# Draining the compressed heads between three projection jobs, letting the first group of heads run on into the second, and dealing the second gate's sums 2, 3, 3, 3, 3, 2

## The chip, the core and the metric

The kernel runs on one core of one Trainium2 chip. The metric is device time in microseconds. Three runs of the kernel before gave 1657.56 us (median), 1658.36 us and 1652.24 us. What a measurement of this kernel can tell from no change is about 0.5%, some 8 us.

## The reference, cut to what matters

One step of a transformer trunk over 128 context tokens and 256 latent tokens (three tiles of 128 rows), width 2048:

```
sh1, sc1, g1, sh2, sc2, g2 = split(silu(cond) @ w_mod + b_mod, 6)        # per condition
z   = modulate(rms_norm(x, g_attn), sh1, sc1) @ w_in                     # one wide projection
A:  6 heads, softmax over all latent keys and the context keys
B:  6 heads, softmax over a band of latent keys, the context keys and a sink
C:  4 heads over a low-rank compressed key/value ("compressed heads")
x   = x + g1 * (concat(o_a, o_b, o_c) @ w_o)
x   = x + g2 * moe(modulate(rms_norm(x, g_ffn), sh2, sc2))               # 32 experts, top 2
```

The six parts of the modulation each take a 2048 x 2048 slice of `w_mod` (16 MB in float32). The change concerns when the attention of C, A and B is drained, and when the slices for the gate g1 (G1), the scale sc2 (SC2) and the gate g2 (G2) are worked off.

## The kernel before, in words

The order of the work is written out by the function `plan()`, which returns one list of steps. Every engine then walks that same list and does its own part of each step; semaphores tie the engines together. An engine never takes a later step before an earlier one, so the place of a step in the list is its place in the queue of each engine.

The kinds of step that matter here:

- `proj`: a projection job, one column chunk of `w_in` for one tile of 128 tokens. TensorE (PE) does 16 matmuls in the program, shown as 32 by the profile (L1263). ScalarE (ACT) squares and copies the result out of the bank and raises `z_ready`; GpSimd (POOL) forms the factor of the norm (L2546, L2498) and raises `rstd_ready`.
- `norm`: VectorE (DVE) scales the job's columns by norm and gain (L2167) and, for latent tiles, rotates them (L1962 to L1967), then raises `norm_ready`.
- `turn`, `cache`: PE transposes the job's result, or the cached keys, into one of two transpose banks (L1304, L1310), and ACT copies them out and raises `tp_read`.
- `qk`: scores of one head and tile (L1323 and L1325 for C, L1329 for A and B); DVE takes the maximum (L2222), ACT the exponential (L1753). `nz`: DVE normalises the probabilities (L2236, L2237). `pt`: PE transposes them into a transpose bank (L1337), ACT copies them out (L1763, L1768).
- `pv`: PE multiplies by the values (L1354). For a compressed head the result goes into the last quarter of the very transpose bank that the same head's `pt` used, and DVE copies it out from there (L2244) and raises `o_ready`. For A and B three heads share one `pv` and a bank of their own (L2246).
- `mod`: PE adds one of the 16 slices of G1 or SC2 (L1121), 1 MB of weights each. After the 16th DVE adds the bias row (L2151), and the first slice of the next part waits for that. `sum`: DVE adds a slice of sh2 itself (L2132). `g2`: DVE adds a slice of G2 itself (L2108).
- `lead`: a quarter of the first tile of the output projection, dealt between the last attention steps. `out`: one tile and column block of the output projection (L1239).

The two transpose banks are used in turn. The function `tp_bank` lets PE into a bank when ACT has read what was there two uses ago; and where that was the `pt` of a compressed head, also when DVE has copied that head's output:

```python
                if n - 2 in output_in:
                    pe.wait_ge(o_ready, pv_units.index(output_in[n - 2]) + 1)
```

Inside `plan()`, `advance(u)` moves the attention pipeline by one: `qk` of a new unit u, then a waiting `pv`, `nz` and `pt` of older ones; `advance()` without a unit drains it by one. `attend(...)` calls it for a list of heads and tiles, with `mod` steps dealt in by `before`, `before_pt`, `before_pv` and `drain`. `mods(n)` takes the next n slices from `later`, a list of 16 of G1 and 16 of SC2.

Weights come by one DMA queue on SyncE, 1 MB units into a ring of 12 slots, in the order in which `plan()` lists them; a unit is requested when the unit 12 places before it has been used. After the attention come the output projection, the router, and the experts in pairs; the loop over pairs (L1533, L1564) fills the time from about 748 us to the end.

Of the kernel before, what the change touches and what calls it, by code (L numbers as in the profile page):

```python
# [26 lines left out]
TILES = 3  # L27
T = TILES * P
KD = D // P
HD = 128  # L30
HEADS_A, HEADS_B, HEADS_C = 6, 6, 4
SHARE = 3
# [83 lines left out]
LATER_GROUPS = (G1, SC2)  # L116
SUMMED = {"aq0": (0, 1, 1), "aq1": (1, 1, 1), "bq0": (1, 1, 1), "akv": (2, 2, 2), "bq1": (1, 1, 0)}
FOLD_LOW = 12
G2_STEPS = (3, 3, 2, 3, 2, 3)
SCALED_AT = {6: (0, 1, 2), 7: (3, 4, 5), 8: (6, 7, 8), 9: (9,), 10: (10,), 11: (11,)}  # L120
FOLD_AT = 6

# [70 lines left out]
def plan():  # L193
# [18 lines left out]
    def mod(g, k):  # L212
        if g == "lead":
            if k == 0:
                units.extend([("out", 0, i) for i in range(4)])
            steps.append((g, k))
            return
        units.append(("mod", g, k))
        if (g, k) == (G1, FOLD_LOW):
            steps.append(("fold", 1))  # L220
        steps.append(("mod", g, k))
# [8 lines left out]
    later = [(g, k) for g in LATER_GROUPS for k in range(KD)]  # L230
    pending = []
    summed = [0]

    def job(kind, what, norm=True):
        jobs.append(what)
        if what == ("akv", 0):
            steps.append(("fold", 0))
        steps.append((kind, len(jobs) - 1))
        for _ in range(SUMMED[what[0]][what[1]] if what[0] in SUMMED else 0):
            units.append(("mod", SH2, summed[0]))  # L240
            steps.append(("sum", summed[0]))
            summed[0] += 1
        if norm:
            steps.append(("norm", len(jobs) - 1))
        if len(pending) == 2:
            steps.append(("turn", pending.pop(0)))
        pending.append(len(jobs) - 1)
# [4 lines left out]
    scored, unnormalised, turned_p = [], [], []  # L252

    def advance(u=None, fill=0, before_pv=0):

        if u is not None:
            steps.append(("qk", u))
            scored.append(u)
        if turned_p:
            mods(before_pv)  # L260
            steps.append(("pv", turned_p.pop()))
        if unnormalised:
            steps.append(("nz", unnormalised.pop()))
        if u is not None:
            unnormalised.append(u)
        if scored and (u is None or len(scored) > 2):
            if unnormalised == [scored[0]]:
                steps.append(("nz", unnormalised.pop()))
            mods(fill)
            done = scored.pop(0)  # L270
            steps.append(("pt", done))
            if atts[done][0] == "C" or atts[done][1] % SHARE == SHARE - 1:
                turned_p.append(done)

    def attend(group, heads, tiles=range(TILES), fill=(), flush=False, drain=(), before=(), before_pt=(), before_pv=()):

        fill = list(fill)
        each = [(h, t) for h in heads for t in tiles] if group == "C" else [(h, t) for t in tiles for h in heads]
        drain = list(drain)
        for n, (h, t) in enumerate(each):  # L280
            if fill:
                mod(*fill.pop(0))
            mods(before[n] if n < len(before) else 0)
            atts.append((group, h, t))
            advance(len(atts) - 1, before_pt[n] if n < len(before_pt) else 0, before_pv[n] if n < len(before_pv) else 0)
        while flush and (scored or turned_p):
            mods(drain.pop(0) if drain else 0)
            advance()

    def mods(n):  # L290
        for g, k in later[:n]:
            mod(g, k)
        del later[:n]
# [3 lines left out]
    def chunk_units(name):  # L297
        units.extend(units_of(name))
# [16 lines left out]
    for name, _, _ in CHUNKS:  # L315
        if name in EARLY + ("cq1", "aq0"):
            continue
        chunk_units(name)
        for t in range(TILES):
            attends = name in ("aq1", "bq1", "bkv") or (name, t) == ("bq0", 0)  # L320
            job("proj", (name, t), norm=not attends)
            n = len(jobs) - 1
            if name == "akv" and t == 0:
                steps.append(("cache", "a"))
            if name == "aq1":
                attend("C", [t])
            if (name, t) == ("bq0", 0):
                attend("C", [TILES], flush=True, drain=(1, 1, 1))
            if name == "bq1":
                if t == 0:  # L330
                    steps.append(("turn", pending.pop(0)))
                    attend("A", range(SHARE), [t], before=(1, 0, 1))
                else:
                    attend("A", range(SHARE), [t], before_pt=(0, 1), before_pv=(0, 0, 1))
            if name == "bkv":
                attend("A", range(SHARE, HEADS_A), [t], before_pt=(0, 1), before_pv=(0, 0, 1))
            if attends:
                steps.append(("norm", n))
    for n in (1, 1, 0):
        mods(n)  # L340
        advance()
    assert not scored and not turned_p
    steps.append(("cache", "b"))
    steps.extend(("turn", n) for n in pending)
    assert summed[0] == KD and KD - 2 < len(later) <= KD
    attend("B", range(SHARE), fill=later[:SHARE * TILES])
    attend("B", range(SHARE, HEADS_B), fill=later[SHARE * TILES:] + [("lead", 0), ("lead", 1)])
    for i in (2, 3):
# [5 lines left out]
    for n, (cc, t) in enumerate(OUT_ORDER):  # L354
        if t == 0 and cc:
            units.extend([("out", cc, i) for i in range(4)])
        steps.append(("out", cc, t))
        for _ in range(G2_STEPS[n] if n < len(G2_STEPS) else 0):
            units.append(("mod", G2, g2_k))
# [51 lines left out]

def build(nc, ins, outs):
    steps, jobs, atts, units = plan()
    lay, n_const = const_layout()
    chunk_at = {name: (at, w) for name, at, w in CHUNKS}
# [2244 lines left out]
```

How the kernel before makes its waits and increments, by code:

```python
        @block.sync  # L897
        def _(sp):
            for t in range(TILES):
                src = ins["x_sample"][0, (t - 1) * P:t * P, :] if t else ins["x_prompt"][0]
                sp.dma_start(xn[:, t, :], src).then_inc(x_in[t], 16)
            for m, u in enumerate(units):
                slot = ring_slot(m)
                if m >= SLOTS:
                    sp.wait_ge(*frees[m - SLOTS])
                src, shape = unit_source(u)
                sp.dma_start(cut(slot, shape), src).then_inc(slot_full[slot], 16)
                if u in EARLY_BEHIND:
                    i, half = divmod(EARLY_BEHIND.index(u), 2)
                    rows = slice(2 * half, 2 * half + 2)
                    if i == 0 and half == 0:
                        sp.wait_ge(ssx_ready, TILES)
                    for c, name in enumerate(EARLY):
                        if i >= 2 and half == 0:
                            sp.wait_ge(early_used, 2 * (i - 2) + c + 1)
# [6 lines left out]
                src, shape = unit_source(("moe0", u))  # L922
                dst = first_place(u)
                if len(shape) > 1:
                    dst = dst.rearrange("p (a b) -> p a b", a=shape[0])
                if u in first_no:
                    sp.wait_ge(*frees[first_no[u] - SLOTS])
                    sp.dma_start(dst, src).then_inc(slot_full[ring_slot(first_no[u])], 16)
                else:
                    if u == EXTRA[1] - 1:
                        sp.wait_ge(mod_done, 2)
                    elif u == EXTRA[0]:
```

## Time and profile before

| | |
|---|---|
| median of three runs | 1657.56 us (1652.24 to 1658.36) |
| profiled execution, device time | 1652.31 us |
| its span in the trace | 1650.2 us |
| PE busy | 1552.4 us, 94% |
| DVE busy | 814.7 us, 49% |
| DMA moved | 581.94 MB |

The device time of the profiled execution is 2.1 us above its span; what changes in the span changes the device time by as much. PE is busy nearly all the time up to about 800 us, with the weight stream below its full rate for much of it; from about 700 us on the DMA engines are full. Where PE stands still is told by the square brackets of the timeline: how long the engine was idle before the row, and who released it.

### The profile page before, as it was taken

To read this page: it belongs to the slowest core of one execution; us is meant where nothing else is said; L and a number is where in the kernel's file an instruction comes from. 1 tells how busy PE (TensorE), PEld (TensorE's weight loads), DVE (VectorE), ACT (ScalarE), POOL (GpSimd) and SP (SyncE) were. 2 spreads that over 40 slices of the span, in tenths; PEclk is the share of its full clock that TensorE was granted. 3 is DMA by queue.
4 is the path that set the end of the run, shared out by engine and by line. 5 is a ranking of instruction groups with operands and counts; after the bars stand their busy time and mean duration, and the time that the engine had idled before them with its cause. 6 is when DMAs were issued, how large, how long until landed. Compare 5 with 4: busy or idle time off the path is not lost.

```text
span 1650.2 us, 18186 instructions
## 1 busy us (share of the span) xinstructions
PE 1552.4 (94%) x6534; PEld 648.0 (39%) x6579; DVE 814.7 (49%) x1473; ACT 282.6 (17%) x748; POOL 101.4 (6%) x185
## 2 busy tenths in 40 slices
PE   6999999999999999999989989988989998988998
PEld 3446655454434444543333233233233233323323
DVE  4774655762365972525525533543443442452544
ACT  3124231122231000111110110111011011011010
POOL 1013100000121001000000000000000000000000
PEclk9999999999999999999999999999999999999999
DMA  9993531567596783899999999999999999999997
GB/s 391 417 411 146 197 135 72 240 235 300 219 391 273 305 319 115 307 412 394 429 426 430 428 426 429 426 428 428 422 428 427 417 428 428 429 426 423 427 426 295
DMA packets 62126, 581.94 MB, mean 353 GB/s; under 512 B 9217, under 2 KB 10177, under 8 KB 16939
## 3 DMA queue, kind: packets, MB, share of 16 engines
q1 hardware_dynamic: 54848, 557.34, 81.7%
q0 software_dynamic: 5936, 23.23, 3.6%
q10 hardware_dynamic: 1296, 0.77, 0.2%
q8 instruction: 27, 0.44, 0.1%
q14 instruction: 19, 0.16, 0.0%
HBM read 584.07 MB, written 7.05 MB: 358 GB/s over the span
## 4 chain that ended last, share of the span: by engine, by line
PE 68%; DMA 16%; DVE 2%; issue 1%; ACT 1%; SPq 0%; POOL 0%; DVEq 0%; ACTq 0%; POOLq 0%
PE bank L1533 23%; DMA ring<-in_w 16%; PE bank L1263 11%; PE bank L1239 9%; PE bank L1436 7%; PE bank L1564 6%; PE bank L1354 2%; PE bank L1485 2%; PE bank L1121 1%; PE bank L1329 1%; PE bank L1583 1%; DVE r L2108 1%; PE bank L1508 1%; PE bank L1337 1%; PE bank L1546 1%
## 5 line engine op out<-in xcount | busy, mean ns | idle before, releaser
L1533 PE MATMUL bank<-ring,r 128*64 128x512 f32 x1920 | 445.5, 600 | 3.9 <-DMA ring<-in_w 3.9
L1564 PE MATMUL bank<-ring,mod_row 128*64 128x512 f32 x896 | 215.5, 637 | 49.9 <-DMA ring<-in_w 42.1
L1533 PEld LDWEIGHTS bank<-ring,r 128*64 128x64 f32 x1920 | 126.2, 136 | 255.8 <-issue 255.7
L1263 PE MATMUL bank<-ring,r 128*128 128x384 f32 (+2 forms) x672 | 225.5, 494 | 0.0
L2373 DVE TENSOR_TENSOR bank<-bank,r 128x512 f32<-128x512 f32 x180 | 125.3, 696 | 105.2 <-PE bank L1436 105.1
L1239 PE MATMUL bank<-ring,r 128*128 128x512 f32 x384 | 170.3, 595 | 1.5 <-issue 1.5
L1263 PEld LDWEIGHTS bank<-ring,r 128*128 128x128 f32 x672 | 123.6, 190 | 91.4 <-issue 43.7
L1564 PEld LDWEIGHTS bank<-ring,mod_row 128*64 128x64 f32 x896 | 78.2, 146 | 177.6 <-issue 167.4
L1436 PE MATMUL bank<-r 128*128 128x512 bf16 x495 | 132.2, 381 | 7.2 <-issue 7.2
L2375 DVE TENSOR_TENSOR r<-r,bank 128x512 f32<-128x512 f32 x180 | 123.7, 687 | 6.2
L2398 DVE TENSOR_SCALAR gains<-bank,w_now 128x512 f32<-128x512 f32 x30 | 22.5, 751 | 206.1 <-PE bank L1564 196.5
L1239 PEld LDWEIGHTS bank<-ring,r 128*128 128x128 f32 x384 | 71.0, 191 | 80.7 <-issue 80.6
L2381 DVE TENSOR_TENSOR gain_row<-gain_row,bank 128x512 f32<-128x512 f32 x16 | 11.0, 689 | 183.7 <-PE bank L1533 167.2
L1436 PEld LDWEIGHTS bank<-r 128*128 128x128 bf16 x540 | 40.6, 97 | 149.5 <-DVE r L2375 86.8
L1059 PE MATMUL bank<-r 128*128 128x512 f32 (+1 forms) x192 | 78.4, 557 | 1.3 <-DVE r L1895 1.1
L2108 DVE SCALAR_TENSOR_TENSOR r<-ring,csil,r 128x2048 f32<-128x2048 f32 x32 | 74.3, 2348 | 4.3 <-DMA r<-in_b_mod 3.8
L2132 DVE SCALAR_TENSOR_TENSOR spare<-ring,csil,spare 128x1024 f32<-128x1024 f32 x60 | 73.1, 1279 | 0.1
L1910 DVE CUSTOM_DVE_ANT_0 r<-ring,r 128x2048 bf16<-128x2048 f32 x28 | 65.8, 2351 | 9.4 <-ACT r L1630 7.4
L2222 DVE TENSOR_REDUCE small<-bank 128x1 f32<-128x384 f32 (+1 forms) x48 | 22.5, 468 | 82.6 <-PE bank L1329 58.8
L1792 ACT ACTIVATE gain_row<-bank 128x512 f32<-128x512 f32 x16 | 9.6, 597 | 308.9 <-PE bank L1533 295.2
L1786 ACT ACTIVATE r<-bank 128x512 f32<-128x512 f32 x30 | 17.8, 595 | 240.5 <-PE bank L1423 240.5
L2167 DVE SCALAR_TENSOR_TENSOR r<-r,small,gains 128x128 f32<-128x128 f32 (+2 forms) x91 | 27.5, 343 | 59.0 <-POOL small L2498 53.4
(306 smaller groups left out, 1279.4 us busy)
## 6 DMA issues: line engine op xcount, KB each, us to landing
ring<-in_w SPq DMA_DIRECT2D x174, 2048.0 KB, 17.8
ring<-in_w_mod SPq DMA_DIRECT2D x48, 1024.0 KB, 14.8
ring<-in_w SPq DMA_DIRECT2D x29, 1024.0 KB, 13.1
ring<-in_w_scale SPq DMA_DIRECT2D x16, 1024.0 KB, 23.5
ring<-in_w_shift SPq DMA_DIRECT2D x16, 1024.0 KB, 21.3
ring<-in_w_low SPq DMA_DIRECT2D x16, 1024.0 KB, 8.5
ring<-in_w_o SPq DMA_DIRECT2D x16, 1024.0 KB, 6.8
r<-mod_d POOLq DMA_DIRECT2D x8, 1024.0 KB, 7.5
```

The lines of the kernel that those rows point to most:

```text
L1059: mm = pe.matmul(early_bank[3 * c + t][:, 0:w], h_t[:, k, t * P:(t + 1) * P], early_w[c][i % 2][:, jj, :], start=(k == 0), stop=(k == KD - 1))
L1239: mm = pe.matmul(acc[acc_of(a)][:, :], qo[:, t, k, :], wu[:, j, :], start=(k == 0), stop=(k == KD - 1))
L1263: mm = pe.matmul(acc[acc_of(a)][:, 0:w], h_t[:, k, t * P:(t + 1) * P], wu[:, j, :], start=(k == 0), stop=(k == KD - 1))
L1354: mm = pe.matmul(out, v, prob_t[u % 2][:, i, :] if g == "C" else prob_ab[batch_of(u) % 2][:, i, :], start=(i == 0), stop=(i == len(tiles) ...
L1436: mm = pe.matmul(y_ps[k % 4][:, :], of_token[:, t * P:(t + 1) * P], y_part[:, n_part, c, :], start=(n_part == 0), stop=(n_part == 2))
L1533: mm = pe.matmul(ps[64 * c:64 * c + 64, :], xg_t[:, j, 64 * c:64 * c + 64], big_cut(slot_of(u), (8, 512))[:, j % 8, :], start=(j == 0), st ...
L1564: mm = pe.matmul(y_ps[c][64 * h:64 * h + 64, :], act_t[:, f, 64 * h:64 * h + 64], big_cut(slot_of(u), (2, D))[:, c % 2, f * 512:(f + 1) * ...
L1910: last = v.tensor_tensor_reduce(junk_s, w, cond_all[:, c, :], 1.0, b_shift[:, k:k + 1], ALU.mult, ALU.add, mod_t[:, 1, k, c:c + 1])
L2108: last = v.scalar_tensor_tensor(out=g2_sum[:, c, :], in0=ring[:, ring_slot(m), :], scalar=csil[:, k, c:c + 1], in1=g2_sum[:, c, :], op0=AL ...
L2132: last = v.scalar_tensor_tensor(out=shift_sum[:, c, :], in0=rows, scalar=by, in1=shift_sum[:, c, :], op0=ALU.mult, op1=ALU.add)
L2373: v.tensor_tensor(ps[:, :], ps[:, :], g2b[:, min(t, 1), cols], ALU.mult).then_inc(strip_scaled, 1)
L2375: return v.tensor_tensor(x1[:, t, cols], x1[:, t, cols], ps[:, :], ALU.add)
```

## The change

Three edits of `plan()` and one of its tables.

```diff
-G2_STEPS = (3, 3, 2, 3, 2, 3)
+G2_STEPS = (2, 3, 3, 3, 3, 2)
...
             n = len(jobs) - 1
+            if (name, t) in (("bq0", 1), ("bq0", 2), ("akv", 0)):
+                advance()
...
             if (name, t) == ("bq0", 0):
-                attend("C", [TILES], flush=True, drain=(1, 1, 1))
+                attend("C", [TILES], before=(1,))
             if name == "bq1":
                 if t == 0:
                     steps.append(("turn", pending.pop(0)))
-                    attend("A", range(SHARE), [t], before=(1, 0, 1))
+                    attend("A", range(SHARE), [t], before=(2, 0, 2))
...
             if name == "bkv":
-                attend("A", range(SHARE, HEADS_A), [t], before_pt=(0, 1), before_pv=(0, 0, 1))
+                attend("A", range(SHARE, HEADS_A), [t], before_pt=(1, 1) if t == 0 else (0, 1), before_pv=(0, 0, 1))
...
-    for n in (1, 1, 0):
-        mods(n)
-        advance()
-    assert not scored and not turned_p
     steps.append(("cache", "b"))
     steps.extend(("turn", n) for n in pending)
```

**The compressed heads' drain.** Before, the last three drain steps stood right behind the last score, each behind a `mod`. Now one `mod` stands ahead of those scores, and the three drain steps stand one each behind the jobs bq0 tile 1, bq0 tile 2 and akv tile 0. What PE does there, before (L1263 a projection, L1304 a job's transposes, L1121 a `mod`, L1354 a `pv`, L1337 a `pt`; banks 4 and 5 are the transpose banks):

```order
L1337 MATMUL bank4<-cst,r3 128x128 [waits p_ready,o_ready,tp_read]
L1121 MATMUL bank3<-ring,csil_low 4x512 [waits z_ready,slot_full5]
L1121 MATMUL bank3<-ring,csil_low 4x512 x3
L1354 MATMUL bank4<-r3 128x128 [waits tp_read]
L1337 MATMUL bank5<-cst,r3 128x128 [waits p_ready,o_ready,tp_read]
L1337 MATMUL bank5<-cst,r3 128x128 x2
L1121 MATMUL bank3<-ring,csil 2x512 [waits slot_full6]
L1121 MATMUL bank3<-ring,csil 2x512 x3
L1354 MATMUL bank5<-r3 128x128 [waits tp_read]
```

Here the `pt` behind a `pv` takes the other bank, and what it waits for is the copy of the head one further back. What PE does now behind job bq0 tile 1 (all lines of the changed kernel stand two lower from here on: L1261, L1302, L1352, L1335):

```order
L1261 MATMUL bank0<-ring,r1 128x384 [waits slot_full3]
L1261 MATMUL bank0<-ring,r1 128x384 x3
L1302 MATMUL bank5<-cst,r3 128x128 [waits norm_ready,o_ready,tp_read]
L1302 MATMUL bank5<-cst,r3 128x128 x2
L1352 MATMUL bank4<-r3 128x128 [waits tp_read]
L1335 MATMUL bank4<-cst,r3 128x128 [waits p_ready,o_ready,tp_read]
L1335 MATMUL bank4<-cst,r3 128x128 x2
L1261 MATMUL bank1<-ring,r1 128x384 [waits slot_full0,z_ready]
```

The job's transpose has come between one head's `pt` and the next, so the next `pt` (L1335) now takes the bank 4 in which the `pv` just before it has written. DVE, before, at the same place (L2244 the copy of a head's output, L2236 and L2237 an `nz`, L2167 the norm of a job):

```order
L2244 COPY r2<-bank5 128x128 [waits o_full]
L2236 RECIPROCAL small<-small 128x1 [waits e_ready]
L2237 TENSOR_SCALAR r3<-r3,small 128x384 [waits v_step]
L2244 COPY r2<-bank4 128x128 [waits o_full]
L2236 RECIPROCAL small<-small 128x1 [waits e_ready]
L2237 TENSOR_SCALAR r3<-r3,small 128x384 [waits v_step]
L2244 COPY r2<-bank5 128x128 [waits o_full]
L2244 COPY r2<-bank4 128x128 [waits o_full]
L2167 SCALAR_TENSOR_TENSOR r3<-r3,small,gains 128x128 [waits rstd_ready,z_ready]
```

All copies stand ahead of the next job's norm. DVE now, behind job bq0 tile 1:

```order
L2165 SCALAR_TENSOR_TENSOR r3<-r3,small,gains 128x128 [waits rstd_ready,z_ready]
L2165 SCALAR_TENSOR_TENSOR r3<-r3,small,gains 128x128 x2
L1960 TENSOR_TENSOR r3<-r3,cst 128x192 [waits v_step]
L1961 TENSOR_TENSOR r3<-r3,cst 128x192
L1962 TENSOR_TENSOR r3<-r3,cst 128x192
L1963 TENSOR_TENSOR r3<-r3,cst 128x192
L1964 TENSOR_TENSOR r3<-r3 128x192 [waits v_step]
L1965 TENSOR_TENSOR r3<-r3 128x192
L2242 COPY r2<-bank4 128x128 [waits o_full]
L2234 RECIPROCAL small<-small 128x1 [waits e_ready]
```

The copy of the head's output (L2242) has moved from ahead of the jobs to behind the norm and the rotation of each of them. The same holds behind bq0 tile 2 and akv tile 0 (whose norm has no rotation, and where the cached keys' transpose takes the bank).

**The first group runs on.** The three drain steps of A with their two `mod` steps ahead of the cached keys' transpose are gone; A's last probabilities are carried along by B's first units, and every `mod` of SC2 stands one unit of B later. The 32 slices are the same; two of G1's come one job later and two more are dealt ahead of A's first scores. The order of what PE does at the end of B, before (L1329 scores, L1239 a `lead`):

```order
L1354 MATMUL bank<-r 128x384 [waits o_ready,cache_v_in,tp_read]
L1337 MATMUL bank<-cst,r 128x128 [waits p_ready,tp_read]
L1337 MATMUL bank<-cst,r 128x128 x2
L1239 MATMUL bank<-ring,r 128x512 [waits slot_full11,o_ready,z_ready]
L1239 MATMUL bank<-ring,r 128x512 x3
L1329 MATMUL bank<-r 128x384 [waits tp_read,e_ready]
L1337 MATMUL bank<-cst,r 128x128 [waits p_ready,tp_read]
L1337 MATMUL bank<-cst,r 128x128 x2
L1239 MATMUL bank<-ring,r 128x512 [waits slot_full0]
```

Behind the last `pv` but one the first `lead` follows at once. Now:

```order
L1352 MATMUL bank<-r 128x384 [waits o_ready,cache_v_in,tp_read]
L1335 MATMUL bank<-cst,r 128x128 [waits p_ready,tp_read]
L1335 MATMUL bank<-cst,r 128x128 x2
L1119 MATMUL bank<-ring,csil 2x512 [waits slot_full10]
L1119 MATMUL bank<-ring,csil 2x512 x3
L1327 MATMUL bank<-r 128x384 [waits tp_read,e_ready]
L1335 MATMUL bank<-cst,r 128x128 [waits p_ready,tp_read]
L1335 MATMUL bank<-cst,r 128x128 x2
L1237 MATMUL bank<-ring,r 128x512 [waits slot_full11,o_ready,z_ready]
```

The last `mod` has moved in ahead of the first `lead`, and each `lead` stands one unit later.

**The second gate's sums.** The 16 sums of G2 on DVE are dealt to the first six tiles of the output projection as 2, 3, 3, 3, 3, 2 where it was 3, 3, 2, 3, 2, 3.

## Rows read from the trace of the kernel before

**Rows 1.** The page: busy us, share of the span and instructions of each engine.

```profile
PE 1552.4 (94%) x6534; PEld 648.0 (39%) x6579; DVE 814.7 (49%) x1473; ACT 282.6 (17%) x748; POOL 101.4 (6%) x185
```

**Rows 2.** Stretches: us, busy per engine, PE clock, DMA share, GB/s.

```profile
310.00:320.00 10.00, 10.00 (x24) 4.37 (x23) 9.90 (x9) 0.00 (x0) 0.69 (x2) 1.00 0.09 31
640.00:650.00 10.00, 10.00 (x33) 5.17 (x32) 5.55 (x6) 1.31 (x3) 2.11 (x3) 1.00 0.15 37
700.00:800.00 100.00, 98.39 (x470) 37.56 (x474) 40.88 (x89) 16.86 (x28) 4.89 (x8) 1.00 0.99 406
```

**Rows 3.** PE timeline, drain and next jobs: start, length, work [idle before, releaser].

```profile
259.58 0.52 PE L1337 MATMUL bank<-cst,r 128*128 128x128 f32 x3 [0.43 <-ACT r L1720]
270.11 0.94 PE L1354 MATMUL bank<-r 128*128 128x128 f32 x6
270.88 10.49 PE L1263 MATMUL bank<-ring,r 128*128 128x384 f32 x32
281.20 0.49 PE L1304 MATMUL bank<-cst,r 128*128 128x128 f32 x3
281.53 10.49 PE L1263 MATMUL bank<-ring,r 128*128 128x384 f32 x32
291.85 0.49 PE L1304 MATMUL bank<-cst,r 128*128 128x128 f32 x3
307.09 0.49 PE L1304 MATMUL bank<-cst,r 128*128 128x128 f32 x3
```

**Rows 4.** DVE timeline, same stretch: an output's copy, then the jobs' norms.

```profile
266.75 0.29 DVE L2244 COPY r<-bank 128x128 f32<-128x128 f32 x1 [0.77 <-PE bank L1354]
283.99 0.88 DVE L2167 SCALAR_TENSOR_TENSOR r<-r,small,gains 128x128 f32<-128x128 f32 x3 [7.05 <-POOL small L2498]
286.38 0.35 DVE L1967 TENSOR_TENSOR r<-r 128x192 f32<-128x192 f32 x1
297.03 0.35 DVE L1967 TENSOR_TENSOR r<-r 128x192 f32<-128x192 f32 x1
309.63 0.61 DVE L2167 SCALAR_TENSOR_TENSOR r<-r,small,gains 128x128 f32<-128x128 f32 x2 [3.62 <-POOL small L2498]
```

**Rows 5.** ACT timeline, job akv tile 0: the copy that waits for all compressed outputs.

```profile
307.81 0.38 ACT L1674 ACTIVATE r<-bank 128x256 f32<-128x256 f32 x1
```

**Rows 6.** PE timeline: first scores of A, and the end of A.

```profile
348.13 0.68 PE L1329 MATMUL bank<-r 128*128 128x128 f32 x4 [0.59 <-ACT r L1741]
444.85 0.49 PE L1337 MATMUL bank<-cst,r 128*128 128x128 f32 x3
448.86 1.04 PE L1121 MATMUL bank<-ring,csil 128*2 128x512 f32 x8 [2.07 <-DVE mod_row L2151]
450.96 2.20 PE L1354 MATMUL bank<-r 128*128 128x384 f32 x6 [0.58 <-ACT r L1768]
```

**Rows 7.** ACT and DVE timelines at the end of A.

```profile
446.01 0.48 ACT L1768 ACTIVATE r<-bank 128x384 f32<-128x384 f32 x1
447.83 0.28 DVE L1967 TENSOR_TENSOR r<-r 128x128 f32<-128x128 f32 x1
```

**Rows 8.** PE timeline: the leads, and the fold of the second gate.

```profile
491.75 3.67 PE L1239 MATMUL bank<-ring,r 128*128 128x512 f32 x8 [1.50 <-issue]
503.16 2.20 PE L1354 MATMUL bank<-r 128*128 128x384 f32 x6 [1.71 <-ACT r L1768]
608.85 1.90 PE L1197 MATMUL bank<-r,cst 128*2 128x512 f32 x16 [0.37 <-DVE r L2108]
```

**Rows 9.** PE timeline in the last stage, behind waits for weights (3 of 13).

```profile
854.81 10.09 PE L1564 MATMUL bank<-ring,mod_row 128*64 128x512 f32 x32 [3.63 <-DMA ring<-in_w]
974.86 7.09 PE L1564 MATMUL bank<-ring,mod_row 128*64 128x512 f32 x32 [3.34 <-DMA ring<-in_w]
1154.93 8.51 PE L1564 MATMUL bank<-ring,mod_row 128*64 128x512 f32 x32 [3.63 <-DMA ring<-in_w]
```

**Rows 10.** The stretch behind the first of these waits; columns as in rows 2.

```profile
856.00:859.00 3.00, 3.00 (x8) 0.79 (x6) 0.00 (x0) 0.00 (x0) 0.00 (x0) 0.50 0.99 421
```

More of the change, by code:

```diff
@@ L335, in plan @@
             if name == "bkv":
-                attend("A", range(SHARE, HEADS_A), [t], before_pt=(0, 1), before_pv=(0, 0, 1))
+                attend("A", range(SHARE, HEADS_A), [t], before_pt=(1, 1) if t == 0 else (0, 1), before_pv=(0, 0, 1))
             if attends:
                 steps.append(("norm", n))
-    for n in (1, 1, 0):
-        mods(n)
-        advance()
-    assert not scored and not turned_p
     steps.append(("cache", "b"))
     steps.extend(("turn", n) for n in pending)
-    assert summed[0] == KD and KD - 2 < len(later) <= KD
+    assert summed[0] == KD and len(later) == KD
     attend("B", range(SHARE), fill=later[:SHARE * TILES])
```

## The prediction

> **What bounds the kernel now.** I read the page first: PE is busy 1552 of 1650 us [rows 1], so the engine that others wait for is PE. Then the table of stretches, to see who limits whom and where: from 700 us on the DMA engines are full at a share of 0.99, before it they mostly are not, 0.09 from 310 to 320 us and 0.15 from 640 to 650 us, while PE is at ten of ten [rows 2]. The weight queue runs dry there because it waits for ring slots that PE (or DVE) has yet to free. So up to the start of the expert stage PE sets the time, and what PE loses or gains there moves the start of the full weight stream and with it the end, one for one. The change works only between 258 and 609 us. Last I read PE's timeline of that stretch for the brackets, and beside each the timelines of DVE and ACT, because an idle bracket of PE is all that an edit of the order can win, and a new one is what it can lose. The work itself is the same: the same jobs, heads, slices and sums.
>
> **The compressed heads' drain: what goes.** In the stretch from 258 to 271 us the only bracket is 0.43 us, in front of a `pt` that waits for ACT's copy of a job's transposes [rows 3]. The `mod` that now stands ahead of the scores covers it. Gain 0.43.
>
> **The drain: what comes.** Behind bq0 tile 1 PE does the transposes of an older job, the `pv` of a compressed head into bank 4, and then the `pt` of the next head into the same bank 4. That `pt` waits for `o_ready`, DVE's copy of the `pv`. DVE takes the copy after the norm of bq0 tile 1, and that norm needs ACT and POOL first. Before, job bq0 tile 1 ends where the next transposes start, at 281.20 [rows 3]. Its norm starts at 283.99 and the last of its rotation ends at 286.38 + 0.35 = 286.73 [rows 4], 5.5 us behind the job. The copy takes 0.29 [rows 4]: `o_ready` comes 5.8 us behind the job. PE has 0.33 us of transposes (281.20 to 281.53 [rows 3]) and some 0.3 of a short `pv`, then stands. New wait: 5.8 - 0.6 = 5.2 us. The same behind bq0 tile 2: the job ends at 291.85 [rows 3], its last rotation at 297.03 + 0.35 = 297.38 [rows 4], again 5.5; the `pv` has three key tiles now, 0.77 (270.11 to 270.88 [rows 3]). New wait: 5.8 - 1.1 = 4.7 us. Behind akv tile 0 it is the cached keys' transpose that wants the bank. The job ends at 307.09 [rows 3], its norm, which has no rotation, at 309.63 + 0.61 = 310.24 [rows 4], 3.15 behind. ACT's copy at 307.81 [rows 5] is held until all compressed outputs are made (k and v of A share their memory); the last `pv` now ends at 307.09 + 0.33 + 0.94 = 308.36 [rows 3], so the chain through ACT, POOL and DVE is 0.55 later. New wait: 3.15 + 0.55 + 0.29 - 1.1 = 2.9 us. Sum 12.8 us. Queued behind the waiting instruction on PE is the next projection job, 10 to 14 us of work with nothing else ready, so nothing hides it. DVE's own sums have room: they do not end later than the next job does. Bounds: the waits could be smaller by what PE's `pv` and transposes take longer, 0.5 us in all, and not below 12; they could be larger by a handoff of 0.1 to 0.2 us each.
>
> **What the clock adds.** How PE's clock answers to a wait shows in the last stage, behind the waits for weights. Behind the first of them, 3.63 us long, the same 32 matmuls take 10.09 us that take 7.09 behind another [rows 9], and the granted clock is 0.50, that is 1.2 of 2.4 GHz, for a stretch behind the wait [rows 10]. Of the 13 such waits of 1.96 to 4.33 us, nine were followed by a longer row, by 1.42 (8.51) to 3.00 (10.09), 1.9 on average; of the six of at least 3.5 us all were [rows 9]. The waits of 5.2 and 4.7 us are longer than any of these and stand in front of a job whose matmuls fill the array, so I charge 1.9 each, 3.8. The third, 2.9 us, lies among the seven shorter ones, of which three were followed by a longer row: 3/7 x 2.1 = 0.9. Together 4.7 us, bounded by 0 and 3 x 3.0 = 9.0. The Trainium skill says the same against this change (page "TensorE: Matmul & The Clock Gate", section "Why this matters for your kernels"): idle gaps between bursts of matmuls put the array back to half its rate. By that rule both long waits cost this; without it the sum would be the waits alone.
>
> **A's first scores.** PE waits 0.59 us at 348.13 for the copy of the last key tile [rows 6]; a second `mod` now stands in between, of about 1 us, and covers it. Gain 0.59. The weights for the two slices moved are requested in the same order as they are used, and the queue has idle time there, so they are not late.
>
> **The end of A.** Two brackets go: 2.07 us where the first slice of SC2 waits for DVE's addition, and 0.58 us before the last `pv` of A [rows 6]. What is late next: the transposes of the last two key jobs now stand directly behind the `pt` at 444.85. The first needs the bank that ACT empties at 446.01 + 0.48 = 446.49 [rows 7], while PE is there at 445.4: 1.1 us. The second needs the norm of the last job, 447.83 + 0.28 = 448.11 [rows 7], while PE would be there at 446.7: 1.4 us. A few tenths more may come before the carried `pv`. So 2.65 go and 2.5 to 2.9 come: 0, between -1 and +1.
>
> **The leads.** The first `lead` waits 1.50 us, and the `pv` behind the second waits 1.71 us for ACT's copy of a `pt` [rows 8]. Now the last `mod` stands ahead of the first `lead`, so the copy of the `pv` that it needs is done; and the second `lead`, 3.6 us, stands between that `pt` and its `pv`. Both go: gain 3.2, or at worst 2.
>
> **The second gate.** PE waits 0.37 us at 608.85 for DVE's last sum [rows 8]. With two sums instead of three in the last part DVE is a whole sum (4.7 us) earlier. Its first part has one less, so the residual that frees a bank comes earlier too. Gain 0.37.
>
> **The sum.** +12.8 - 0.43 - 0.59 + 0 - 3.21 - 0.37 = +8.2 us of waits, +4.7 of clock: +12.9 us. On the profiled execution of 1652.31 us that gives 1665.2. The median of the runs shown, 1657.56, is 5.3 above it, and the four times there are lie two at 1652.3 and two near 1658; from the median the sum is 1670.5. I take the middle, 1668.
>
> **Rivals.**
> The clock holds. All waits come as worked out but the matmuls behind them run at full rate: +8.2, which is 1660.5 to 1665.8, middle 1663. For it: four of the 13 rows were not longer. Against it: those were all behind shorter waits.
> The delay is repaid. If the expert stage were bound by weights that arrive at fixed times, PE could be late at 700 us and wait less at each of its 13 waits there. Then the time stays where it was, 1655 to 1659. Against it: the queue moves 37 GB/s at 640 us because its slots are not free [rows 2], so the stream itself starts later by the same amount.
> Faster. If PE between 310 and 440 us were paced by arriving weights rather than by itself, it would stand for weights less by just what it comes late; all that is lost before 310 us (12.8 + 4.7 - 0.43 = 17.1) would be won back by 440 us, and the gains outside it, 0.59 + 3.21 + 0.37 = 4.2, would remain: 1648.1 from the profiled execution, 1653.4 from the median, middle 1651. It decides the sign once 17.1 - 4.2 = 12.9 us are won back there. Against it: a DMA share of 0.09 at 310 us with PE at ten of ten [rows 2], and no bracket but the 0.59 [rows 6] at which it could win.
> Worse. The third wait throws the clock too and each fall costs 3.0, as the dearest row shows [rows 9]: +8.2 + 9.0 = +17.2, 1669.5 to 1674.8.
>
> **Numbers.** The forecast has 60%, the clock that holds 15%, the repaid delay 11%, worse 9%, faster 5%. About 0.5%, 8 us, is what a measurement of this kernel can tell from no change. Slower by more than that: all of the forecast and of the worse case, and some half of the holding clock, since +8.2 lies on the bound: 76%. Within it: the repaid delay, the other half of the holding clock, and of the faster case what is measured from the median (-4.2): 20%. Faster by more than that: the faster case where its runs fall on the lower of the two bases (9.5 below the median): 4%. The range: the forecast's own goes from +10 to +15 on either base, 1662 to 1673; it is widened to take in the holding clock and part of the worse case, 1657 to 1678.
>
> **What would show it.** In the changed kernel's PE timeline: brackets of about 5.2, 4.7 and 2.9 us at L1335, L1335 and L1308, each released by DVE's copy L2242; a granted clock of 0.50 in the stretch behind the first two and a projection row longer than 10.49 us; no bracket at the first scores of A, none of 1.5 or more at the leads; two brackets of 1 to 1.5 us at the transposes of the last key jobs; the DMA share still 0.99 from some 710 us on. The prediction is wrong if the copy is not the releaser or these brackets are below 1 us, if the clock stays at 1.00 behind them, or if the expert stage is shorter by what the front is longer.

## The result, and the profile after

| | before | changed |
|---|---|---|
| median of 6 runs | 1656.26 us (1652.24 to 1658.36) | 1667.30 us (1664.33 to 1668.96) |
| ratio | | 1.0065, 95% interval 1.0054 to 1.0077 |
| profiled execution, device time | 1652.31 us | 1665.41 us |
| its span | 1650.2 us | 1663.3 us |

The changed kernel is 0.65% slower, 11.0 us by the medians and 13.1 us by the two spans: the profiled execution before lies 4.0 us below its median, that of the changed kernel 1.9. The forecast was 1668 us.

The page shows that PE has become busier and not less so. The row that answers to [rows 1]:

```profile
PE 1567.1 (94%) x6579; PEld 651.8 (39%) x6579; DVE 814.3 (49%) x1473; ACT 282.8 (17%) x748; POOL 101.4 (6%) x185
```

The same work is 14.7 us more of busy time. Matmuls that run at half the clock count as busy, and some records are missing before (6534 against 6579), so this line tells nothing of waits; the timeline does. PE where [rows 3] stood, from the job bq0 tile 1 (L1261 a projection job, L1302 a job's transposes, L1352 a `pv`, L1335 a `pt`, L1308 the cached keys' transposes):

```profile
276.92 0.39 PE L1352 MATMUL bank<-r 128*128 128x128 f32 x2
282.41 0.87 PE L1335 MATMUL bank<-cst,r 128*128 128x128 f32 x3 [5.11 <-issue]
283.08 11.77 PE L1261 MATMUL bank<-ring,r 128*128 128x384 f32 x32
...
295.01 0.83 PE L1352 MATMUL bank<-r 128*128 128x128 f32 x6
300.51 0.87 PE L1335 MATMUL bank<-cst,r 128*128 128x128 f32 x3 [4.67 <-issue]
301.32 1.89 PE L1128 MATMUL bank<-spare,cst 128*4 128x256 f32 x16
303.14 15.47 PE L1261 MATMUL bank<-ring,r 128*128 128x512 f32 x32
...
322.38 0.41 PE L1308 MATMUL bank<-cst,r 128*128 128x128 f32 x2 [2.77 <-issue]
322.63 15.60 PE L1261 MATMUL bank<-ring,r 128*128 128x512 f32 x32
```

Three brackets of 5.11, 4.67 and 2.77 us stand where there was none, and the job behind the first takes 11.77 us where it took 10.49 [rows 3]. Who releases the brackets the profile does not name ("issue": it saw no event). DVE's timeline does, beside [rows 4]:

```profile
279.37 0.88 DVE L2165 SCALAR_TENSOR_TENSOR r<-r,small,gains 128x128 f32<-128x128 f32 x3 [6.63 <-POOL small L2496]
...
282.03 0.28 DVE L2242 COPY r<-bank 128x128 f32<-128x128 f32 x1
...
300.13 0.28 DVE L2242 COPY r<-bank 128x128 f32<-128x128 f32 x1
...
322.00 0.28 DVE L2242 COPY r<-bank 128x128 f32<-128x128 f32 x1
```

Each time the copy of the `pv` (L2242) ends 0.10 us before PE goes on: 282.31 and 282.41, 300.41 and 300.51, 322.28 and 322.38. The `pv` itself had ended at 277.31; DVE stood idle 6.63 us in front of the norm and then did the whole rotation before the copy. The clock behind the three waits (columns as in [rows 2]):

```profile
283.00:286.00 3.00, 3.00 (x8) 1.66 (x7) 3.00 (x3) 0.49 (x1) 0.00 (x0) 0.56 0.00 0
301.00:304.00 3.00, 3.00 (x19) 0.92 (x18) 0.73 (x2) 0.49 (x1) 0.00 (x0) 0.50 1.00 423
322.00:325.00 3.00, 2.62 (x6) 1.33 (x7) 3.00 (x5) 0.38 (x1) 0.53 (x1) 0.70 0.33 93
```

The clock falls behind all three. The granted clock is 0.56, 0.50 and 0.70 in them, and 0.50 is 1.2 of 2.4 GHz. Summed from PE's rows: behind the first wait the `pt` takes 0.35 longer (0.87 against 0.52 in [rows 3]) and the job 1.28; behind the second the `pt` 0.35, the fold at L1128 0.84 and the job 1.47, against the 1.05 and 14.00 us that they take where the clock holds (the first experiment below); behind the third the job 1.70 (13.90). That is 1.6 + 2.7 + 1.7 = 6.0 us.

What was to go at the other places of [rows 6 to 8]. PE at A's first scores, at the end of A, and at the leads (L1237):

```profile
363.19 1.90 PE L1119 MATMUL bank<-ring,csil 128*2 128x512 f32 x16
...
465.13 0.44 PE L1302 MATMUL bank<-cst,r 128*128 128x128 f32 x2 [0.98 <-ACT r L1766]
466.86 0.66 PE L1302 MATMUL bank<-cst,r 128*128 128x128 f32 x2 [1.29 <-DVE r L1965]
467.45 1.89 PE L1119 MATMUL bank<-ring,csil 128*2 128x512 f32 x8
...
473.68 2.20 PE L1352 MATMUL bank<-r 128*128 128x384 f32 x6 [0.16 <-ACT r L1766]
...
517.82 2.10 PE L1352 MATMUL bank<-r 128*128 128x384 f32 x6
```

The 0.59 at the scores is gone, and so are the 1.50 and the 1.71 at the leads. At the end of A 2.65 us went and 0.98 + 1.29 + 0.16 = 2.43 came. But the clock falls here as well, for the fourth time: the `mod` behind the two waits takes 1.89 us, where the same `mod` takes 1.04 in [rows 6], and the granted clock is 0.50

```profile
467.00:469.00 2.00, 2.00 (x10) 0.22 (x10) 0.00 (x0) 0.38 (x1) 1.99 (x3) 0.50 1.00 415
```

Of the eight kernels here in which A runs on, seven show this fall; in the last experiment (slices in the waits) the clock holds behind the same two waits. From the start of the second waiting row to the start of the last `pv` of A, its own bracket of 0.16 left out, PE takes 6.66 us here and 5.39 there, so this fall costs 1.3 us. Brackets and clock together, the end of A has not come out even: it costs about 1.0 us.

One measure serves all kernels below: the stretch of PE from the first transposes in front of the drain to the row in which the shift vectors are made (L1178, x64). Before it runs from 257.60 to 515.93, 258.33 us. The changed kernel's runs from 257.63 to 530.49: 272.86 us, 14.5 longer. Behind it the changed kernel takes 1132.8 us and the one before 1134.3, so 1.5 us come back there; 0.37 of it is the bracket in front of the second gate's fold, which is gone, and 0.8 is less waiting for weights in the expert stage (41.3 us against 42.1, 13 waits each).

### The profile page after: what moved, and what is told of

Read it like the earlier page. It is cut to its first block, busy times and chain, and to the rows that moved or that the text cites. A ratio compares the mean times of both kernels' runs of the same rounds, so it can differ in the third digit from the quotient of the medians.

```text
span 1663.3 us, 18231 instructions
## 1 busy us (share of the span) xinstructions
PE 1567.1 (94%) x6579; PEld 651.8 (39%) x6579; DVE 814.3 (49%) x1473; ACT 282.8 (17%) x748; POOL 101.4 (6%) x185
## 4 chain that ended last, share of the span: by engine, by line
PE 70%; DMA 16%; issue 1%; ACT 1%; DVE 1%; SPq 0%; POOL 0%; DVEq 0%; ACTq 0%; POOLq 0%
PE bank L1531 22%; DMA ring<-in_w 16%; PE bank L1261 11%; PE bank L1237 10%; PE bank L1434 7%; PE bank L1562 6%; PE bank L1483 2%; PE bank L1352 2%; PE bank L1119 1%; PE bank L1327 1%; PE bank L1581 1%; PE bank L1506 1%; PE bank L1335 1%; PE bank L1544 1%; PE bank L1215 1%
## 5 line engine op out<-in xcount | busy, mean ns | idle before, releaser
L1562 PE MATMUL bank<-ring,mod_row 128*64 128x512 f32 x896 | 215.5, 637 | 49.2 <-DMA ring<-in_w 41.3
L1261 PE MATMUL bank<-ring,r 128*128 128x384 f32 (+2 forms) x672 | 229.9, 501 | 0.0
L1237 PE MATMUL bank<-ring,r 128*128 128x512 f32 x384 | 170.3, 595 | 0.0
L1261 PEld LDWEIGHTS bank<-ring,r 128*128 128x128 f32 x672 | 125.6, 193 | 94.4 <-issue 47.2
L1434 PE MATMUL bank<-r 128*128 128x512 bf16 x540 | 142.4, 382 | 0.0
L1237 PEld LDWEIGHTS bank<-ring,r 128*128 128x128 f32 x384 | 71.0, 191 | 79.0 <-issue 78.9
## 6 DMA issues: line engine op xcount, KB each, us to landing
ring<-in_w_mod SPq DMA_DIRECT2D x48, 1024.0 KB, 15.5
```

The source lines that it names most:

```text
L1237: mm = pe.matmul(acc[acc_of(a)][:, :], qo[:, t, k, :], wu[:, j, :], start=(k == 0), stop=(k == KD - 1))
L1261: mm = pe.matmul(acc[acc_of(a)][:, 0:w], h_t[:, k, t * P:(t + 1) * P], wu[:, j, :], start=(k == 0), stop=(k == KD - 1))
L1434: mm = pe.matmul(y_ps[k % 4][:, :], of_token[:, t * P:(t + 1) * P], y_part[:, n_part, c, :], start=(n_part == 0), stop=(n_part == 2))
L1562: mm = pe.matmul(y_ps[c][64 * h:64 * h + 64, :], act_t[:, f, 64 * h:64 * h + 64], big_cut(slot_of(u), (2, D))[:, c % 2, f * 512:(f + 1) * ...
```

## The experiments

Each run is given by its median over the median of the kernel before on the same chip, with the 95% interval, and by its "stretch" as defined above (before 258.3, changed 272.9).

**The copy ahead of the norm.** At the three jobs the drain step comes between the job and its norm, so DVE's copy stands ahead of the norm; PE's order stays the same.

```diff
-            job("proj", (name, t), norm=not attends)
+            drains = (name, t) in (("bq0", 1), ("bq0", 2), ("akv", 0))
+            job("proj", (name, t), norm=not (attends or drains))
...
-            if (name, t) in (("bq0", 1), ("bq0", 2), ("akv", 0)):
+            if drains:
                 advance()
+                steps.append(("norm", n))
```

> The changed kernel with one thing different: each of the three drain steps stands between its job and the job's norm, so VectorE copies the head's output before the norm. PE's order and the banks are as in the changed kernel. Theory (PE waits for a copy that VectorE takes behind the norm): the three waits of 5.11, 4.67 and 2.77 us shrink to 0.3 to 0.5 us each, the clock stays at 1.00 between 270 and 330 us, the three jobs behind take 10.5, 14.0 and 13.9 us again, and the span falls by 11 (waits) and 6 (clock), to about 1646 us; 4 us below the kernel before. Rival (the shared bank alone costs it, whatever VectorE's order): the waits stay at 4 us and more and the span at 1660 us.

Measured: 0.9968 (0.9956 to 0.9980), stretch 255.8. PE's timeline:

```profile
278.81 0.52 PE L1337 MATMUL bank<-cst,r 128*128 128x128 f32 x3 [0.43 <-issue]
279.16 10.49 PE L1263 MATMUL bank<-ring,r 128*128 128x384 f32 x32
...
291.08 0.52 PE L1337 MATMUL bank<-cst,r 128*128 128x128 f32 x3 [0.43 <-issue]
291.52 1.05 PE L1130 MATMUL bank<-spare,cst 128*4 128x256 f32 x16
292.50 14.00 PE L1263 MATMUL bank<-ring,r 128*128 128x512 f32 x32
...
307.93 0.41 PE L1310 MATMUL bank<-cst,r 128*128 128x128 f32 x2 [0.43 <-issue]
308.18 13.90 PE L1263 MATMUL bank<-ring,r 128*128 128x512 f32 x32
```

The three waits are 0.43 us each: the copy (L2244) ends 0.33 us behind the end of its `pv`, and PE goes on 0.10 behind that; and the jobs behind them run at full rate. The bank rule of PE is untouched, so it is DVE's place for the copy that costs. The 0.43 of [rows 3] has the same cause: the copy there ends at 259.48 and PE goes on at 259.58, again 0.10 later. The span of this execution is 1647.3 us, where about 1646 was expected.

**The old drain with the rest of the change.** The compressed heads end as before; everything behind akv stays changed.

```diff
-            if (name, t) in (("bq0", 1), ("bq0", 2), ("akv", 0)):
-                advance()
...
-                attend("C", [TILES], before=(1,))
+                attend("C", [TILES], flush=True, drain=(1, 1, 1))
...
-                    attend("A", range(SHARE), [t], before=(2, 0, 2))
+                    attend("A", range(SHARE), [t], before=(1, 0, 1))
```

> The changed kernel with the compressed heads' drain and the slices around it as in the kernel before; the first group still runs on, and the sums are dealt anew. Theory: none of the three waits, and the gains at the leads (3.2 us) and at the fold (0.37) remain: a span of about 1646.5 us against 1650.2, 3.7 us faster than the kernel before (0.2%). Rival (the delay of the drain was in part made by the other two edits): the span stays above 1650.

Measured: 0.9968 (0.9955 to 0.9980), stretch 255.5, that is 2.8 below before. The end of A, the leads and the gate are together a gain of 0.3%, the fall of the clock at the end of A included, which this kernel has too (0.50 from 453 to 455 us). The first scores' bracket, 0.58 us here, is back as in [rows 6]. The span is 1647.8 us, 1.3 more than expected.

**The drain alone.** The kernel before with the first edit of the drain and the `before=(2, 0, 2)` that belongs to it, without the other parts.

```diff
+            if (name, t) in (("bq0", 1), ("bq0", 2), ("akv", 0)):
+                advance()
...
-                attend("C", [TILES], flush=True, drain=(1, 1, 1))
+                attend("C", [TILES], before=(1,))
...
-                    attend("A", range(SHARE), [t], before=(1, 0, 1))
+                    attend("A", range(SHARE), [t], before=(2, 0, 2))
```

> The kernel before with the drain's part of the change alone (drain steps behind the three jobs, slices 1 and 2, 0, 2 around them). Theory: the three waits of 5.1, 4.7 and 2.8 us and the falls of the clock behind them (6 us), less 1.0 gained: a span of 1650.2 + 12.6 + 6.1 - 1.0 = 1667 to 1668 us, 1.0% slower than before, 4 to 5 us slower than the whole change. Rival (the expert stage gives part of the delay back): less than 12 us slower.

Measured: 1.0114 (1.0097 to 1.0131), stretch 275.8. PE's timeline:

```profile
285.11 0.87 PE L1339 MATMUL bank<-cst,r 128*128 128x128 f32 x3 [5.11 <-issue]
285.78 13.06 PE L1265 MATMUL bank<-ring,r 128*128 128x384 f32 x32
...
304.50 0.77 PE L1339 MATMUL bank<-cst,r 128*128 128x128 f32 x3 [4.66 <-issue]
```

The third wait is 2.77 again, and all three are the same as in the changed kernel to 0.01 us. The first job took 13.06 us here and 11.77 in the changed kernel, behind the same wait: what a fall costs differs from one execution to the next. By the stretch the drain costs 17.5 us and the other parts save 2.8, sum 14.7, against 14.5 measured with both. By the medians the two are 18.9 us slower and 5.3 us faster, sum 13.6, against 11.0. The span missed its forecast: 1671.0 us in place of 1667 to 1668, for the most part because this execution comes to the drain 2.7 us late (last section). The rival, less than 12 us slower, is excluded.

**Matmuls in the waits.** Between the `pv` and the waiting instruction PE does 14, 13 and 7 more matmuls of 128x384, whose result nobody reads.

```diff
-                advance()
+                advance(warm={("bq0", 1): 14, ("bq0", 2): 13, ("akv", 0): 7}[name, t])
...
+                elif s[0] == "warm":
+                    pe.wait_ge(e_ready, 12)
+                    for _ in range(s[1]):
+                        pe.matmul(sc_ps[0][:, 0:384], h_t[:, 0, 0:P], h_t[:, 0, 0:384], start=True, stop=True)
```

> The changed kernel with 14, 13 and 7 matmuls of 128x384 more, whose result nobody reads, put on PE between each of the three outputs and the instruction that waits (0.33 us each: 4.6, 4.3 and 2.3 us, less than the waits). Theory (the clock falls because PE stands idle, and the fall costs some 6 us): the waiting instructions start as late as before behind their jobs (5.7, 5.7 and 3.9 us), the clock stays at 1.00, the jobs behind take 10.5, 14.0 and 13.9 us, and the span is about 6 us shorter than the changed kernel's, 1657 us. Rival (the longer jobs behind the waits have another cause, as the weight stream that fills at that time): they stay at 11.8, 15.5 and 15.6 us and the span at 1663.

Measured: 1.0085 (1.0071 to 1.0098), stretch 275.9. I had sized them wrong: one such matmul of the program is two rows of the profile, 0.65 us in all, so they filled twice the time and ran past the end of the waits:

```profile
277.79 9.20 PE L1289 MATMUL bank<-r 128*128 128x384 f32 x28
...
287.15 10.49 PE L1263 MATMUL bank<-ring,r 128*128 128x384 f32 x32
```

The jobs behind ran at full rate. The span, 1667.3 us, is far from the 1657 expected, but the overrun can be taken off: the three instructions behind start 3.8, 3.6 and 1.6 us later behind their `pv` than in the changed kernel, 8.9 in all, and the stretch is only 3.0 longer. That leaves 5.9 us saved, about as much as the three falls cost. It was done again with half as many.

**Half as many.** The same with 7, 6 and 3.

> The changed kernel with 7, 6 and 3 matmuls of 128x384 more, whose result nobody reads, between each of the three outputs and the instruction that waits. One such matmul of the program is two rows of the profile and took 0.65 us in the run with 14, 13 and 7, which was twice what had been meant; now they are 4.5, 3.9 and 1.9 us, less than the waits. Theory (the falls of the clock are paid for standing idle and cost 6 us): the waiting instructions start as late behind their jobs as in the changed kernel (5.8, 5.8 and 3.9 us), the clock stays at 1.00, the jobs behind take 10.5, 14.0 and 13.9 us, and the span is 6 us below the changed kernel's 1663.3: 1657 to 1658. Rival (something else makes those jobs long): span 1663.

Measured: 1.0029 (1.0017 to 1.0041), stretch 267.4.

```profile
279.62 0.39 PE L1358 MATMUL bank<-r 128*128 128x128 f32 x2
279.85 4.68 PE L1289 MATMUL bank<-r 128*128 128x384 f32 x14
285.12 0.52 PE L1341 MATMUL bank<-cst,r 128*128 128x128 f32 x3 [0.59 <-issue]
285.47 10.49 PE L1263 MATMUL bank<-ring,r 128*128 128x384 f32 x32
```

The wait is as long as ever (the `pt` starts 5.1 us behind the end of the `pv`), but PE stands idle for only 0.59, 0.79 and 0.83 us in the three, and the granted clock is 1.00 in every stretch from 282 to 324. The stretch is 5.5 us shorter than the changed kernel's, the ratio 0.36 points lower, which is 6.0 us (3 to 9 by the two intervals). The span, 1660.4 us, is above the 1657 to 1658 expected, since this execution too comes to the drain 2.7 us late. So of some 18.5 us that the drain's new place costs (12.55 of waits and 6.0) the clock is a third: a wait on this path costs more than its length.

**The drain step ahead of norm and turn.** At the three jobs the drain step comes directly behind the job, before its norm and before the older job's transposes.

```diff
+        if what in (("bq0", 1), ("bq0", 2), ("akv", 0)):
+            advance()
...
-            if (name, t) in (("bq0", 1), ("bq0", 2), ("akv", 0)):
-                advance()
```

> The changed kernel with each of the three drain steps directly behind its projection job, ahead of that job's norm and of the older job's transposes. VectorE copies the output before the norm, and PE does not come back to the bank at once. Theory: waits of at most 0.43 us in place of 5.11, 4.67 and 2.77; no fall of the clock; within 1 us of the kernel that only moved the copy ahead of the norm, a span of 1646 to 1647, ratio to before 0.996 to 0.997. Rival (the job's transposes are now the late ones, because the norm of the job before is held up): new waits of over 1 us at the transposes.

Measured: 0.9961 (0.9947 to 0.9974), stretch 255.5, the lowest ratio of all kernels here, though its interval overlaps those of the first two experiments. PE's timeline:

```profile
277.51 0.49 PE L1334 MATMUL bank<-cst,r 128*128 128x128 f32 x3
278.11 0.52 PE L1301 MATMUL bank<-cst,r 128*128 128x128 f32 x3
278.46 10.49 PE L1260 MATMUL bank<-ring,r 128*128 128x384 f32 x32
...
290.05 0.52 PE L1334 MATMUL bank<-cst,r 128*128 128x128 f32 x3 [0.43 <-issue]
```

Behind the first job the `pt` has the other bank and waits for nothing; the older job's transposes want the `pv`'s bank, and its copy, ahead of the norm on DVE, holds them up by 0.1 us at most (278.11, the `pt` ends at 278.00). Behind the second job the transposes stand between the two `pt`, so the next `pt` has the `pv`'s bank again and waits 0.43, and so do the transposes behind the third. Its stretch and that of the old drain differ by less than 0.1 us: between these two, where the drain's steps lie makes no difference, as long as the copy is not behind the norm.

**The drain step between norm and turn.** One edit other than the last: the step stands behind the norm, yet ahead of the older job's transposes.

> The changed kernel with the drain step behind the job's norm, as it is there, but ahead of the older job's transposes, so that the next head's transpose takes the other bank and only the job's transposes come back to the bank of the output. Theory (it is the copy behind the norm that is late, whoever asks for the bank): the wait moves from the head's transpose to the job's transposes behind it and keeps 4.8, 4.6 and 2.5 us or so; the clock falls as before; a span of 1661 to 1664 us. Rival (it is PE's coming back to the same bank at once that costs): the waits are gone and the span is near 1647.

Measured: 1.0061 (1.0048 to 1.0074), stretch 275.2.

```profile
277.40 0.49 PE L1334 MATMUL bank<-cst,r 128*128 128x128 f32 x3
283.01 0.87 PE L1301 MATMUL bank<-cst,r 128*128 128x128 f32 x3 [5.12 <-issue]
...
301.45 0.87 PE L1334 MATMUL bank<-cst,r 128*128 128x128 f32 x3 [5.00 <-issue]
```

The first `pt` is free and the wait of 5.12 us has only gone over to the transposes (L1301). The second wait did not move, against the expectation: the `pt` there has the `pv`'s bank as before and waits 5.00 us. The third, 2.77 us, is at the transposes. Whoever asks for that bank next pays, and the order on PE alone cures nothing. The span is 1666.9 us where 1661 to 1664 was expected; the fall at the end of A costs 2.9 us in this execution in place of 1.3.

**Slices in the waits.** Four slices of the first gate that stood at A's first scores move into the first two waits (two each), where each is 1 us of useful work.

```diff
-                advance()
+                advance(fill=0 if name == "akv" else 2)
...
-                    attend("A", range(SHARE), [t], before=(2, 0, 2))
+                    attend("A", range(SHARE), [t], before=(0, 0, 0))
```

> The changed kernel with four slices of the gate moved from around A's first scores into the first two waits, two each, between the output and the transpose that waits. Theory: the waiting transposes start as late behind their jobs as before (5.8 us), so 3.9 us of work are done inside the waits; the waits left are 3.1, 2.7 and 2.8 us; the 0.59 us wait at A's first scores comes back; the clock falls behind one or two of them instead of three. Span 1663.3 - 3.9 + 0.6 less 0 to 4 of clock: 1656 to 1660. Rival (the waiting instruction is later by the work put ahead of it): span 1663 and more.

Measured: 1.0054 (1.0041 to 1.0068), stretch 269.8. PE's timeline:

```profile
282.54 0.64 PE L1335 MATMUL bank<-cst,r 128*128 128x128 f32 x3 [3.28 <-issue]
282.97 12.10 PE L1261 MATMUL bank<-ring,r 128*128 128x384 f32 x32
...
300.74 0.52 PE L1335 MATMUL bank<-cst,r 128*128 128x128 f32 x3 [2.84 <-issue]
...
302.16 14.00 PE L1261 MATMUL bank<-ring,r 128*128 128x512 f32 x32
...
362.38 0.68 PE L1327 MATMUL bank<-r 128*128 128x128 f32 x4 [1.56 <-ACT r L1739]
363.90 0.49 PE L1327 MATMUL bank<-r 128*128 128x128 f32 x2 [0.84 <-ACT r L1751]
...
364.64 12.24 PE L1261 MATMUL bank<-ring,r 128*128 128x384 f32 x32
```

The waits shrink by 1.83 each, to 3.28 and 2.84; behind the second the clock now holds, behind the first and the third it still falls. But the place that the slices left needed them: 1.56 + 0.84 us come there, and the job behind them takes 12.24 us where such a job takes 10.49: a fourth fall. Of the 3.7 us of waits and the 2.7 of the fall behind the second that are saved, 2.4 + 1.75 are given back; the 2.2 that stay and the 1.3 of the fall at the end of A, which this execution does not have, come to 3.4, and the stretch is 3.1 us shorter. The span of 1661.7 us lies above the 1656 to 1660 expected. The expectation took the 0.59 us of [rows 6] for the wait at A's first scores, where one slice had still stood ahead of them, and left the clock there out.

## Why the prediction was right, point by point

- **Who bounds.** PE was right. The delay went through to the end: 14.5 us in the stretch, 13.1 in the span. The rivals "repaid" and "faster" are excluded, since PE waits 13 times for weights in the expert stage as before (41.3 us in all). In the kernel before these waits were 42.1 us, so at most 0.8 us of the delay was repaid there. The DMA share from 700 us on came later than I had said, 0.94 over 700 to 800 us and 0.97 over 710 to 810.
- **The three waits.** Forecast 5.2, 4.7 and 2.9, measured 5.11, 4.67 and 2.77. The copy behind the norm as cause is shown by the first and the sixth experiment, which take it away in two ways, and by the seventh, which moves the first wait and does not shorten it.
- **The clock.** Forecast 4.7; measured 6.0 behind the three waits and 1.3 more at the end of A, 7.3 in all. The mechanism was right and the term for the third wait too small: I gave it 3/7 of 2.1, and it fell in the changed kernel, in the drain alone, between norm and turn and with the slices, each time behind 2.77 or 2.78 us, for 1.6 to 1.7 with the waiting row. Matmuls in the waits took the three falls away and 5.5 to 6.0 us with them: shown. The rule of the Trainium skill ("TensorE: Matmul & The Clock Gate", section "Why this matters for your kernels"), that idle gaps put the array back to half its rate, agrees with the 0.50 in the rows above. "The clock holds" is excluded; "worse" had its third fall, but at 1.7 and not 3.0.
- **The 0.43.** Wrong. I put it to ACT's copy of a job's transposes, which a `mod` would cover. It is still there, 0.43 <- issue at 260.77, and it shows in the first and sixth experiment wherever a `pv` and the next taker of its bank stand close. The profile's releaser had named the wrong engine: in the kernel before ACT's copy ends at 259.45, 0.03 us ahead of DVE's, and so looked like the cause; in the changed kernel ACT's ends at 259.47 and the `pt` still waits until 260.77, 0.10 behind DVE's copy.
- **A's first scores, the leads, the end of A.** 0.59 and 3.21 went as said. The end of A was put at 0 as a sum of brackets, and as brackets it is -0.2. What the prediction had at nothing, without a reason, is the clock there: two waits of 0.98 and 1.29 us, as forecast, but with a fall behind them that costs 1.3. With it the end of A is at about +1, the upper bound given. The old drain with the rest of the change shows these as a stretch 2.8 us shorter and a ratio of 0.9968.
- **The second gate.** The 0.37 is gone. Behind the stretch the three parts bring 1.5 us in the profile; kernels without this edit take 1134.3 and 1134.8 there, those with it 1132.7 to 1134.2. That more than 0.37 of this is the edit was not shown.
- **The sum.** +12.9 forecast, +13.1 measured by span. That it is this close is partly luck: the clock was 2.6 dearer and the 0.43 stayed, and the part behind the stretch gave 1.1 more than it was charged. The rows of the stretch leave 1.0 us open as well: the brackets of PE (17.0 us against 8.7 before) and the four falls come to +15.5, and the stretch is 14.5 longer. Where that 1.0 lies stays open.

## What to carry to other kernels

When a step of one pipeline is dealt into the gaps of another, follow what it issues on every in-order queue: here a 0.29 us copy landed behind a norm that itself waited for two other engines, and a bank stayed taken for 5 us. A wait in front of a dense job costs its length and, where the clock falls, more: here 0.3 to 0.6 of the length again behind the three waits of the drain. Waits of about 1 us that stand close together can do it too, so price the clock at every place where brackets come, and not only at the longest. Fill a wait with real work only if the place that gives the work up does not then stand still. If a bracket ends in "issue", or names an engine that the order of the banks does not ask for, look for the semaphore's setter in the other engines' timelines at that very time.

## What the runs showed of the hardware that was not expected

- The first 257 us, the same work in all these kernels, vary by 2.7 us between executions: the drain starts at 257.60 before, at 257.63 in the changed kernel, and at 260.33 in the drain alone and in the kernel with half as many matmuls. At 210 us these two are 1.1 us late; the other 1.6 to 1.7 come behind a wait of 0.92 us that stands in every kernel at that place. The kernel before there, a row of PE's timeline and then one of the stretches (columns as in [rows 2]):

```profile
209.84 0.91 PE L1323 MATMUL bank<-r 128*128 128x384 f32 x2 [0.92 <-ACT r L1753]
```

```profile
213.00:216.00 3.00, 3.00 (x11) 1.81 (x10) 3.00 (x6) 0.25 (x2) 0.00 (x0) 1.00 0.01 3
```

In the drain alone the same bracket, and then a clock of 0.52:

```profile
210.93 0.91 PE L1325 MATMUL bank<-r 128*128 128x384 f32 x2 [0.92 <-ACT r L1755]
```

```profile
213.00:216.00 3.00, 3.00 (x6) 1.66 (x6) 2.93 (x9) 0.84 (x3) 0.00 (x0) 0.52 0.00 0
```

The same wait of the same length lets the clock fall in one execution and not in another. This is a share of what spreads the runs of one kernel, and the reason for measuring by the stretch.
- The same wait of 5.11 us cost 1.6 us of clock in one execution and 2.9 in another; a wait of 2.84 us cost none while one of 2.77 cost 1.7; and a pair of 1.56 and 0.84 us, with 0.68 us of work between, was followed by a fall.
- The pair of 0.98 and 1.29 us at the end of A, with 0.44 us of work between, was followed by a fall in seven kernels, for 1.3 to 1.4 us in six of them and 2.9 in the seventh, and by none in the kernel with slices in the waits. In the kernel before and in the drain alone the waits of 2.07 and 0.58 us there were followed by none. Why the clock held in these three was not found.
